# Compressed attention of two decoder layers: from the first attention loop into the last projection tiles

## The reference, cut to what matters

```python
h = rmsnorm(x, norm_mix); proj = h @ w_in            # q_a k_a v_a f_a q_b kv_b g_b gate_a gate_b
o_a = fox_attention(q, k, v, log_f)                  # 8 heads, full causal, with a forget bias
kc = partial_rope(compress_blocks(kc, ...)); vc = compress_blocks(vc, ...)   # 31 blocks of 32 tokens, MLP with gelu
# nsa_attention, per block of 128 queries (t = 0..3), 8 heads in 2 groups:
s = einsum(q, kc) * scale
valid_c = cmp_end[None, :] <= qpos[:, None]
p_c = softmax(where(valid_c, s, NEG_BIG)) * valid_c  # "compressed" probabilities, 128 x 8 x 31
o_c = p_c @ vc                                       # plus selected and window attention, o_s and o_w
o_n = g0 * o_c + g1 * o_s + g2 * o_w
mixed = sigmoid(gate_a) * y_a + sigmoid(gate_b) * y_b
x = x + mixed @ w_out;  x = x + square(relu(rmsnorm(x) @ w_up)) @ w_down
```

## Time and profile before

| | us |
|---|---|
| median of 3 runs (2207.32 to 2209.14) | 2207.7 |
| the profiled execution | 2207.42 |
| its span, first to last instruction | 2205.6 |
| PE busy | 2181.2 (99%) |
| DVE busy | 1177.8 (53%) |
| ACT busy | 608.8 (28%) |
| POOL busy | 1496.0 (68%) |
| first attention loop of layer 0, from its start to the first gate tile | 778.1 to 823.3 |

### The profile page before, as it was taken

One profiled execution on the slowest core, in us unless ns is written; L12 is line 12 of the kernel. 1 busy time (PEld: TensorE's weight loads), 2 busy tenths in 40 slices (PEclk: granted clock), 3 DMA queues, 4 the chain that ended last, 5 costly groups with the idle time before them and its releaser, 6 DMA issues.

```text
span 2205.6 us, 29834 instructions
## 1 busy us (share of the span) xinstructions
PE 2181.2 (99%) x10952; PEld 1731.9 (79%) x10953; DVE 1177.8 (53%) x1960; ACT 608.8 (28%) x1441; POOL 1496.0 (68%) x679
## 2 busy tenths in 40 slices
PE   8999999999999999999999999999999999999998
PEld 6876788888887767778888888877677788888887
DVE  8769667774455285547650243562765477411423
ACT  5238322221011165531220121111555412200210
POOL 7660687778876614449887888766334397887884
PEclk9999999999999999999999999999999999999999
DMA  5320233333334311113333333333111233333332
GB/s 193 115 77 1 68 95 98 100 99 96 105 92 129 122 30 50 57 58 97 95 98 100 98 96 96 96 115 115 58 40 58 58 90 92 104 97 96 95 96 77
DMA packets 56073, 195.81 MB, mean 89 GB/s; under 512 B 7441, under 2 KB 9489, under 8 KB 55697
## 3 DMA queue, kind: packets, MB, share of 16 engines
q1 hardware_dynamic: 54224, 189.42, 28.4%
q10 hardware_dynamic: 1728, 4.68, 0.6%
HBM read 191.85 MB, written 2.10 MB: 88 GB/s over the span
## 4 chain that ended last, share of the span: by engine, by line
PE 92%; DVE 5%; ACT 1%; issue 1%; DMA 0%; POOL 0%; SPq 0%; DVEq 0%
PE bank L520 26%; PE bank L522 26%; PE bank L521 26%; PE bank L688 3%; PE bank L698 3%; PE bank L735 1%; DVE t L1426 1%; PE bank L717 1%; PE bank L738 1%; DVE prow L1551 1%; PE bank L576 1%; PE bank L645 1%; DVE bank L1540 1%; ACT prow L1144 1%; DMA w_raw<-wstream 0%
## 5 line engine op out<-in xcount | busy, mean ns | idle before, releaser
L465 POOL TENSOR_TENSOR w_hi<-w_raw,zero 128x1024 fp32r<-128x1024 f32 x336 | 651.4, 1939 | 659.4 <-PE bank L522 648.6
L468 POOL TENSOR_TENSOR w_lo<-w_raw,w_hi 128x1024 fp32r<-128x1024 f32 x336 | 845.7, 2517 | 26.4
L520 PE MATMUL bank<-hn_hi,w_hi 128*128 128x512 f32 x1632 | 649.4, 398 | 4.0 <-POOL w_lo L468 2.2
L522 PE MATMUL bank<-hn_hi,w_lo 128*128 128x512 f32 x1632 | 636.6, 390 | 0.0
L521 PE MATMUL bank<-hn_lo,w_hi 128*128 128x512 f32 x1632 | 635.7, 390 | 0.0
L520 PEld LDWEIGHTS bank<-hn_hi,w_hi 128*128 128x128 f32 x1632 | 306.5, 188 | 73.1 <-issue 5.2
L522 PEld LDWEIGHTS bank<-hn_hi,w_lo 128*128 128x128 f32 x1632 | 306.3, 188 | 65.4
L521 PEld LDWEIGHTS bank<-hn_lo,w_hi 128*128 128x128 f32 x1632 | 306.8, 188 | 61.4 <-issue 1.4
L520 PE MATMUL bank<-hid_hi,w_hi 128*128 128x512 f32 x672 | 261.4, 389 | 0.0
L521 PE MATMUL bank<-hid_lo,w_hi 128*128 128x512 f32 x672 | 261.4, 389 | 0.0
L522 PE MATMUL bank<-hid_hi,w_lo 128*128 128x512 f32 x672 | 261.4, 389 | 0.0
(11 more groups left out here) (319 smaller groups left out, 2694.2 us busy)
## 6 DMA issues: line engine op xcount, KB each, us to landing
w_raw<-wstream SPq DMA_DIRECT2D x352, 512.0 KB, 3.6
x<-xT SPq DMA_DIRECT2D x4, 512.0 KB, 7.6
out<-yout SPq DMA_DIRECT2D x12, 128.0 KB, 1.9
mem_x<-memT SPq DMA_DIRECT2D x1, 1024.0 KB, 12.3
lnc<-lncount ACTq DMA_DIRECT2D x1, 1024.0 KB, 6.0
cs<-trig ACTq DMA_DIRECT2D x2, 512.0 KB, 4.3
par<-params ACTq DMA_DIRECT2D x1, 696.0 KB, 5.3
bc<-bconst ACTq DMA_DIRECT2D x1, 664.0 KB, 7.2
```

The lines of the kernel that those rows point to most:

```text
L465: nc.gpsimd.tensor_tensor(w_hi[:, slot, :], w_raw[:, slot, :], zeros, ALU.add).then_inc(w_rounded, 1)
L468: nc.gpsimd.tensor_tensor(w_lo[:, slot, :], w_raw[:, slot, :], w_hi[:, slot, :].bitcast(f32), ALU.subtract).then_inc(w_split, 1)
L520: nc.tensor.matmul(ps[bank][:, 0:cols_], wh, a_h, start=c == 0, stop=False)
L522: mm = nc.tensor.matmul(ps[bank][:, 0:cols_], wl, a_h, start=False, stop=c == chunks - 1)
```

## The change

The compressed scores, softmax and transposes of both layers leave the first attention loop and go into the projection tiles 20 to 25. On PE the scores of t = 0, 1, 2, 3 stand in tiles 20, 21, 23, 24 after five of eight chunks, the transposes in tiles 21, 23, 24, 25 after two chunks. They use bank 5 (free after the rotation at i = 18) in place of bank 3. ACT's copy and exponential stand at the head of its work for tile i, ahead of its copy of that tile; DVE's shift and scale of block t stand together, ahead of scale() of that tile. The block that makes kc stands ahead of scale(19). crow moves to another address. The wait for c_kept stands ahead of the attention.

```diff
+        CMP_SCORED = {20: 0, 21: 1, 23: 2, 24: 3}
+        CMP_TURNED = {21: 0, 23: 1, 24: 2, 25: 3}
...
@@ PE, attend() @@
-                    if g % 2 == 0 and g:
-                        compressed_turn(u0, g // 2 - 1)
                     if g >= 2:
                         group_values(j - 8)
-                    if g % 2 == 0:
-                        compressed_scores(u0, g // 2)
...
                 scores(un, u0, freed, 4)
-                compressed_turn(u0, 3)
                 turn(un - 2, u0)
-                pe.wait_ge(c_kept, TT * (LIN_OF[u0] + 1))
...
@@ PE, compressed_scores() @@
-                    pe.wait_ge(*took(last_on_bank[3]))
+                    pe.wait_ge(cmp_kept, 2 * LIN_OF[u0] + 1)
...
@@ PE, projection tiles; the job after a w1 half @@
-                        linear(jobs[i], hn_hi, hn_lo, S, DC, part=(0, 4))
+                        linear(jobs[i], hn_hi, hn_lo, S, DC, part=(0, 2))
+                        if i in CMP_TURNED:
+                            compressed_turn(u0, CMP_TURNED[i])
+                        linear(jobs[i], hn_hi, hn_lo, S, DC, part=(2, 4))
                         finish(i - 2)
-                        linear(jobs[i], hn_hi, hn_lo, S, DC, part=(4, DC))
+                        linear(jobs[i], hn_hi, hn_lo, S, DC, part=(4, 5))
+                        if i in CMP_SCORED:
+                            compressed_scores(u0, CMP_SCORED[i])
+                        linear(jobs[i], hn_hi, hn_lo, S, DC, part=(5, DC))
...
@@ PE, the other jobs (15 and 25: turned alike, after two chunks) @@
-                        linear(jobs[i], hn_hi, hn_lo, S, DC)
+                        linear(jobs[i], hn_hi, hn_lo, S, DC, part=(0, 2))
+                        if i in CMP_TURNED:
+                            compressed_turn(u0, CMP_TURNED[i])
+                        linear(jobs[i], hn_hi, hn_lo, S, DC, part=(2, 5))
+                        if i in CMP_SCORED:
+                            compressed_scores(u0, CMP_SCORED[i])
+                        linear(jobs[i], hn_hi, hn_lo, S, DC, part=(5, DC))
...
-                pe.wait_ge(cmp_kept, 2 * l + 1)
+                pe.wait_ge(c_kept, TT * (l + 1))
...
@@ ACT, projection tiles, ahead of the work on tile i (removed from attend()) @@
+                    if i in CMP_TURNED:
+                        compressed_keep(FIRST["fox", l], CMP_TURNED[i])
+                    if i in CMP_SCORED:
+                        compressed_exp(FIRST["fox", l], CMP_SCORED[i])
...
@@ DVE, projection tiles, ahead of scale() (removed from attend(); the kc block moved up) @@
+                    if i == 19:
+                        ...
+                    if i in CMP_SCORED:
+                        if i == 20:
+                            link(V.memset(cprob[:, :, NCMP:32], 0.0))
+                        compressed_shift(FIRST["fox", l], CMP_SCORED[i])
+                        compressed_scale(FIRST["fox", l], CMP_SCORED[i])
                     if i < len(jobs) and jobs[i] in SCALED:
                         scale(jobs[i])
```

More of the change, by code:

```diff
@@ L140, in build @@
         s8 = at("s8", [5, TT, 8], f32, R + 56 * KIB + 896)
-        crow = at("crow", [256], f32, R + 62 * KIB)
+        crow = at("crow", [256], f32, R + 54 * KIB)
         cprob = at("cprob", [8, 32], f32, R + 63 * KIB)
@@ L837, in compressed_scores @@
                 if t == 0:
-                    pe.wait_ge(*took(last_on_bank[3]))
+                    pe.wait_ge(cmp_kept, 2 * LIN_OF[u0] + 1)
                 else:
                     pe.wait_ge(c_kept, done)
-                nc.tensor.matmul(ps[3][:, 0:8 * NCMP], identb, cmask[:, t, :], start=True, stop=False)
+                nc.tensor.matmul(ps[5][:, 0:8 * NCMP], identb, cmask[:, t, :], start=True, stop=False)
                 for pair in range(4):
-                    both = ps[3][:, 0:8 * NCMP].rearrange("p (g s n) -> p g s n", g=2, s=4)[:, :, pair, :]
+                    both = ps[5][:, 0:8 * NCMP].rearrange("p (g s n) -> p g s n", g=2, s=4)[:, :, pair, :]
                     mm = nc.tensor.matmul(both, qb[:, pair, t * P:(t + 1) * P], kc[:, :, :], start=False, stop=pair == 3)
@@ L937, in _ @@
                 ph = LIN[l]
+                u0 = FIRST["fox", l]
                 jobs = ph["in"]
@@ L1021, in _ @@
                         mm.then_inc(cmp_out, 1)
-                pe.wait_ge(cmp_kept, 2 * l + 1)
-                u0, u1 = FIRST["fox", l], FIRST["nsa", l] + len(UN)
+                pe.wait_ge(c_kept, TT * (l + 1))
+                u1 = FIRST["nsa", l] + len(UN)
                 attend(u0, FIRST["nsa", l], first_free, ph["gates"], [pair[0] for pair in ph["mix"]])
@@ L1210, in compressed_keep @@
                 act.wait_ge(c_turned, TT * LIN_OF[u0] + t + 1)
-                A(cprobT[:, t, :], ps[3][:, 0:256], ACT.Copy).then_inc(c_kept, 1)
+                A(cprobT[:, t, :], ps[5][:, 0:256], ACT.Copy).then_inc(c_kept, 1)
             norm_first(0, x, hn_hi)
@@ L1507, in compressed_shift @@
                 dve.wait_ge(c_scored, TT * LIN_OF[u0] + t + 1)
-                sc = ps[3][:, 0:8 * NCMP].rearrange("p (h n) -> p h n", h=8)
+                sc = ps[5][:, 0:8 * NCMP].rearrange("p (h n) -> p h n", h=8)
                 mn = cmpc[:, 0, t, :]
@@ L1583, in attend @@
                         write_output(j - 8, *group_output(j - 8), 2 * P)
[L1584 to L1587, removed]
                     scale_rows(j + 2)
@@ L1819, in _ @@
                                                op1=ALU.subtract).then_inc(rope_split, 1)
+                    if i == 19:
+                        dve.wait_ge(cmp_rot, l + 1)
+                        for g in range(2):
+                            cs_ = [csc[:, n, 0:NCMP] for n in range(2)]
+                            sl = slice(g * NCMP, (g + 1) * NCMP)
+                            link(V.tensor_tensor(tmp[:, 0, sl], t1[:, sl], cs_[0], ALU.mult))
+                            link(V.tensor_tensor(tmp[:, 1, sl], ps[5][:, sl], cs_[1], ALU.mult))
+                            rows = slice(64 * g, 64 * g + 64)
+                            ins = V.tensor_tensor(kc[rows, g, :], tmp[rows, 0, sl], tmp[rows, 1, sl], ALU.add)
+                        ins.then_inc(cmp_kept, 1)
+                    if i in CMP_SCORED:
[3 more added lines that the diff above has]
+                        compressed_scale(FIRST["fox", l], CMP_SCORED[i])
                     if i < len(jobs) and jobs[i] in SCALED:
@@ L1889, in _ @@
                         V.tensor_scalar(t1[:, 0:62], ps[4][:, 0:62], pcol(f"b2_k{l}"), None, ALU.add).then_inc(cmp_biased, 1)
[L1890 to L1900, removed]
                 attend(FIRST["fox", l], FIRST["nsa", l], ph["gates"])
```

9 lines of the change are left out of this document (2 added, 7 removed).

## The result

The changed kernel takes 2220.1 us (median of 5 runs, 2219.5 to 2220.7) against 2207.7 for the kernel before (2207.3 to 2209.1): ratio 1.0055, 95% interval 1.0044 to 1.0066. It is slower, as forecast, but by 12.4 us and not by 8.6, and 0.6 us above the range. The profiled execution has a span of 2218.9 us, 13.3 above that of before.

What follows compares the result with a forecast made beforehand. TensorE was taken as the bound (92% of what ended last). Per layer 4.9 inserts + 2.9 stall + 0.5 copy - 4.0 attention gain = +4.3, both layers +8.6: 2216.3 us, range 2207.5 to 2219.5.

Steps and rivals of the forecast that it cites:

- Attention gain: In the attention loop, compressed work taken off DVE and PE brings a pair to 9.42 us: 4.0 us gained per layer.
- Rival 2: Attention becomes DVE's alone, 8.4 us per pair, gain 7.0 per layer: 2205.8 us, or 2203.2 with cheap inserts; chance 0.18.
- Rival 3: Attention hardly moves, ACT's chain or stored outputs take over: gain 1.5 us per layer, 2221.3 us; chance 0.05.
- Inserts: In the projection tiles, where PE has no hole, moved small matmuls cost 0.11 us each: 4.9 us per layer.
- Stall: PE waits for c_prob of t = 0 while two DVE multiplies are locked out by POOL's weight split: 2.9 us per layer.
- rival 1: DVE beats POOL at t = 0, only one multiply waits: stall 0.65 instead of 2.9 us, 2211.8 us; chance 0.24.
- t = 2 not caught: For t = 2 DVE's last multiply starts 0.03 us ahead of POOL: no stall, or 0.9 us if POOL is first.
- The copy: Scores of t = 2 wait for ACT's copy of t = 1, queued behind the last value tile's copy: 0.5 us per layer.

Runs made afterwards that it cites:

- e4: Changed kernel with compressed scores, softmax, transposes and copies left out in both layers, nothing put elsewhere: 2199.4 us, ratio 0.9966.
- e6: Changed kernel with only PE's inserted masks, scores and transposes; the softmax and copy work of DVE and ACT, and PE's waits for it, left out: 2209.6 us.
- e3: Changed kernel with the softmax's sum and reciprocal weight in PSUM bank 5, so L1532 and L1536 have one SBUF operand each: 2210.6 us, ratio 1.0015.
- e1: Changed kernel with the scores of t = 0 after two chunks of tile 20 instead of five: 2210.7 us.
- e5: Changed kernel with ACT's copy of t = 1 moved ahead of its copy of the last value tile: 2218.9 us.
- e9: Kernel of e3 with 8 extra DVE reductions over a PSUM bank before the last multiply of t = 0, making PE wait without the lock: 2218.5 us.
- e10: Kernel of e3 with 6 extra DVE reductions over a PSUM bank before the last multiply of t = 0: 2216.7 us.
- e7: Changed kernel with only the reciprocal weight in a PSUM bank, so L1536 has one SBUF operand and L1532 keeps two: 2214.2 us.
- e8: Changed kernel with the edits of e3 and e5, and block 3 back in the attention after the second group's transposes: 2209.3 us, ratio 1.0006.

## Why the prediction missed, point by point

- **Attention gain, 4.0 per layer: right.** 4.15 and 4.11 by the stages, 4.1 by e4. A pair is 9.25, not 9.42: a little of the wait of 0.45 that was kept in the sum went too. Rival 2 (a pair of 8.4) is refuted; DVE's 8.42 of busy time in the pair is just that figure, but PE's 9.24 now sets it. Rival 3 (1.5 per layer) is refuted as well; that its 2221.3 is the number nearest to the measured 2220.1 is chance.
- **Inserts, 4.9 per layer: right,** 5.1 measured (e6 less e4). The price is 0.115 per matmul, not 0.11.
- **Stall, 2.9 per layer: the mechanism right, the size 3.3 in layer 0 and 3.1 in layer 1.** With S at 743.86, POOL begins at S+2.41 (forecast 2.38), L1532 at S+2.54 (2.43), L1536 ends at S+6.99 (6.8). DVE sees the scores 0.1 later than the rows of the attention suggested, and in layer 0 the transposes ran at the lower clock. POOL is ahead by 0.13 us, so rival 1 is refuted; the forecast had 0.05, less than the 0.1 by which its times are off, so the side of the race was as much luck as reading. e3 (operands) and e1 (moment) both take the stall away.
- **t = 2 not caught: right, by 0.02 us, which is luck.** It is POOL that is longer here, 2.15 where the earlier trace rows have 1.89 (DVE's and POOL's timeline of after):

```profile
768.66 0.42 DVE L1536 TENSOR_TENSOR cprob<-cprob,cmpc 128x248 f32<-128x248 f32 x1
...
768.68 2.15 POOL L467 TENSOR_TENSOR w_hi<-w_raw,zero 128x1024 fp32r<-128x1024 f32 x1 [4.90 <-PE bank L524]
```

  For t = 1 the multiply takes 2.15 from 759.38, and PE is not late, as forecast.
- **The copy, 0.5 per layer: right,** 0.44 (e5).
- **The step that failed: the clock is no term of the sum.** The prediction prices the stall at its own length and puts nothing behind it: PE goes on at full speed, as in every row of before, where the granted clock is 1.00. At the two stalls it fell to 0.50: that cost 2.6 us in layer 0 and 1.7 in layer 1, what the stages leave over (11.39 less 5.1, 3.3 and 0.44, and 10.36 less 5.1, 3.1 and 0.44). Those 4.3 are the bulk of the 4.7 us by which the spans' difference, 13.3, exceeds the sum of 8.6. The stall was 0.6 longer than forecast and the inserts 0.4 dearer; attention and copy give 0.4 back, and 0.2 lie outside these stages. By the medians the clock is 3.2 of the 3.8 us that were missed, and without it the time would be 2216.9, close to the 2216.3 and inside the range. The range ended 0.6 too low for the same reason: no rival had a wait that costs more than it lasts.

The Trainium skill's page "TensorE: Matmul & The Clock Gate", section "HAM oscillation — how this bites in real kernels", warns of idle gaps of PE in the middle of a kernel. The trace agrees with its direction (0.50 behind the stalls of 3.3 us). No rule for the length that brings the fall can be read from the runs here.

What stays open: in which execution a wait brings the fall. e9 and e10 show that the same wait does both, and e7 that a fall comes without a wait as long as these (the longest idle time in the 4.5 us before it is 1.13 us).

## What to carry to other kernels

Work moved from one stage to another where the same engine is full is paid for there; here it cost more than it gave: 8.2 us gained, 10.1 paid. Before a softmax is put beside a POOL that splits weights, look which of its operations have both operands in SBUF, and either put one operand into a PSUM bank or start early enough. And price a wait of a PE that was full as its own length plus the chance of a stretch at half the clock behind it.

## What the runs showed of the hardware that was not expected

- A wait of PE of 3.3 us came with 6.8 us (layer 0) and 3.4 us (layer 1) at a granted clock of 0.50, and with 3.4 us in both layers in e5. One of 3.4 us (e9) and one of 2.5 us (e10) brought 3.4 us in one layer of two, one of 1.3 us (e7) none.
- The clock also fell at the start of layer 0's attention, after 4.5 us in which PE was busy for 3.20 (e7). It did so in the profiled executions of e1, e7, e8 and e10, and in no other. The same 4.5 us have PE busy for 3.19 in before and in e3, with the same 24 matmul records, and there the clock holds: the program alone doesn't decide it. That such falls make the spread of the kernels without a stall (e3: seven runs at 2210.2 to 2210.8, three at 2211.3 to 2212.2) would fit, but is not shown; the kernel before has runs at 2207.3 and at 2209.1 too, and no such fall in its profiled execution.
- DVE's scaling of a fox unit (one 128x128 input in SBUF and a column of factors) waits for POOL too, by its times. In the profiled execution of e8, just before the attention, two of them took 3.49 us, where two take 0.48 in e3's attention beside an idle POOL. The second starts at 782.6 and ends at 784.58, just after two of POOL's instructions that end at 782.60 and 784.50 (DVE's and POOL's timeline). PE waits for both (1.8 us), and the fall in e8's attention, 6.8 us long, comes behind it; that execution (2212.3) is the slowest of e8's eleven:

```profile
781.09 3.49 DVE L1576 TENSOR_SCALAR prow<-prow,cols 128x128 f32<-128x128 f32 x2
...
780.20 2.40 POOL L473 TENSOR_TENSOR w_lo<-w_raw,w_hi 128x1024 fp32r<-128x1024 f32 x1
782.60 1.90 POOL L470 TENSOR_TENSOR w_hi<-w_raw,zero 128x1024 fp32r<-128x1024 f32 x1
```
